# Grams made in turn for both heads, the state's steps put behind the inverse's products, and work placed anew between stages

## The reference

```python
def step(state, inp):                                  # 16 heads of 64, 512 tokens in order
    r_t, w_t, k_t, v_t, a_t, b_t = inp
    sa = jnp.einsum('bhvk,bhk->bhv', state, a_t)
    state = (state * w_t[:, :, None, :] + sa[..., None] * b_t[:, :, None, :]
             + v_t[..., None] * k_t[:, :, None, :])
    return state, jnp.einsum('bhvk,bhk->bhv', state, r_t)
# then, for each head and token:
y = (y - mean) * lax.rsqrt(var + GN_EPS) * ln_w + ln_b + bonus      # mean, var over the 64 of the head
out = y * g
```

## Time and profile before

| | |
|---|---|
| median of 3 runs | 3053.47 us (3048.03 to 3055.04) |
| the profiled execution | 3045.99 us, span 3044.2 us |
| TensorE busy | 2761.3 us (91%) |
| VectorE busy | 2143.8 us (70%) |
| ScalarE busy | 1238.6 us (41%) |
| GpSimd busy | 936.7 us (31%) |
| mean granted TensorE clock | 0.934 of full |

### The profile page before, as it was taken

One profiled execution on the slowest core, in us unless ns is written; L12 is line 12 of the kernel. 1 busy time (PEld: TensorE's weight loads), 2 busy tenths in 40 slices (PEclk: granted clock), 3 DMA queues, 4 the chain that ended last, 5 costly groups with the idle time before them and its releaser, 6 DMA issues. The chain is left out here.

```text
span 3044.2 us, 53724 instructions
## 1 busy us (share of the span) xinstructions
PE 2761.3 (91%) x20933; PEld 1742.6 (57%) x21115; DVE 2143.8 (70%) x3855; ACT 1238.6 (41%) x2050; POOL 936.7 (31%) x563
## 2 busy tenths in 40 slices
PE   8896998978999999999979999958888887889998
PEld 4443455655677777777745566636766664344444
DVE  6793469998788888888866367746667762577743
ACT  4333334478333333333340367634444432343321
POOL 0762344510555555555410222132333321000000
PEclk9657999999999999999989999978999988999999
DMA  4006434567999999999743322031111113623221
GB/s 143 28 1 220 151 118 149 178 243 276 385 374 365 365 359 358 367 364 363 260 152 95 96 74 60 16 137 35 57 34 34 35 55 125 240 83 111 84 104 49
DMA packets 277672, 513.25 MB, mean 169 GB/s; under 512 B 19376, under 2 KB 166448, under 8 KB 275312
## 3 DMA queue, kind: packets, MB, share of 16 engines
q1 hardware_dynamic: 240624, 376.48, 36.4%
q0 software_dynamic: 36864, 134.23, 11.3%
HBM read 445.05 MB, written 65.60 MB: 168 GB/s over the span
## 5 line engine op out<-in xcount | busy, mean ns | idle before, releaser
L1829 PE MATMUL banks<-gated_lo,v_hi 128*128 128x384 bf16 (+2 forms) x1536 | 335.0, 273 | 0.0
L1829 PE MATMUL banks<-gated_hi,v_lo 128*128 128x384 bf16 (+2 forms) x1536 | 335.0, 273 | 0.0
L1829 PE MATMUL banks<-gated_hi,v_hi 128*128 128x384 bf16 (+2 forms) x1536 | 335.0, 273 | 0.0
L1667 POOL DMA_INDIRECT gathered_u<-in_u_rows,first_tile_rows x128 | 212.3, 1659 | 299.2 <-DVE gathered_dots L1775 157.2
L1672 POOL DMA_INDIRECT gathered_v<-in_v,first_tile_rows x128 | 175.3, 1370 | 201.6 <-DVE x_tokens L1767 181.8
L2470 POOL MEMSET between<- 128x2048 bf16 x48 | 86.7, 1805 | 320.5 <-PE banks L3151 320.5
L1829 PEld LDWEIGHTS banks<-gated_hi,v_hi 128*128 128x128 bf16 x1536 | 150.2, 98 | 55.6
L1816 PE MATMUL banks<-act_hi,u_hi 128*128 128x384 bf16 x512 | 168.1, 328 | 12.0 <-DVE u_lo L1753 12.0
L1737 ACT CAST gated_hi<-gated 128x384 bf16<-128x384 f32 x128 | 65.5, 512 | 253.0 <-DVE gated L1789 242.0
L1767 DVE SCALAR_TENSOR_TENSOR x_tokens<-gathered_v,gathered_weights,x_tokens 128x1024 f32<-128x1024 f32 x128 | 164.1, 1282 | 6.1 <-issue 1.8
L1187 PE MATMUL banks<-act_hi,early_u_hi 128*128 128x384 bf16 x512 | 168.3, 329 | 0.0
(11 more groups left out here) (593 smaller groups left out, 7611.2 us busy)
## 6 DMA issues: line engine op xcount, KB each, us to landing
shared_room<-in_u SPq DMA_DIRECT2D x128, 512.0 KB, 3.9
shared_hi<-in_v SPq DMA_DIRECT2D x64, 512.0 KB
shared_lo<-in_v SPq DMA_DIRECT2D x64, 512.0 KB
gate_tables<-gate_piece SPq DMA_DIRECT2D x12, 2048.0 KB, 8.6
gate_group<-gate_tables SPq DMA_DIRECT2D x32, 768.0 KB
late_raw<-in_ffn_up SPq DMA_DIRECT2D x22, 1024.0 KB, 7.2
early_gelu<-early_gelu_columns SPq DMA_DIRECT2D x64, 192.0 KB, 1.9
gelu_early_rows<-early_gelu SPq DMA_DIRECT2D x32, 384.0 KB
```

The costliest lines, as they stand in the source:

```text
L1667: pool.indirect_dma_start(gu[:, n % GROUP, :], None, u_table, bass.IndirectOffsetOnAxis(ap=rows.index[:, 0, n:n + 1], axis=0)).then_inc(gu ...
L1829: m = pe.matmul(ps[:, bank, to:to + width], v[:, j, cols], w[:, j, tok:tok + width], start=start and n == 0 and to == 0, stop=stop and n = ...
```

## The change

1. **GateParts**: the 16 pieces are laid 2, 2, 3, 3, 6 beside chunks 1 to 5, where they were 6, 0, 2, 4, 4.
2. **NSA's output** is stored in eight pieces of two columns as they are made, not in two at the end.
3. **The squash block** is merged into `rwkv_heads`. SP issues the low-rank columns, then `load_pair(0)`, then the tables. TensorE waits for the squashed columns and for the tables only at `norm(0)`.
4. **Grams**: both heads of a gram in turn into two banks (head a SMALL, head b BETWEEN), behind `xlx` of level 2 (gram 1), 3 (gram 0) and 4 (gram 2). VectorE takes head b first. `lx` of levels 3, 4, 5 waits for that.
5. **State's steps**: part 2s-3 now stands behind `lx(s)` and part 2s-2 behind `xlx(s)`, on TensorE, and on ScalarE and VectorE behind the casts that belong to them. Part 11 stands at the end of the pass.
6. **The last pass's end** is done chunk by chunk between the state's steps (new part "last").

```diff
@@ GateParts
-        return {1: range(0, 6), 3: range(6, 8), 4: range(8, 12), 5: range(12, self.count)}.get(c, ())
+        return {1: range(0, 2), 2: range(2, 4), 3: range(4, 7), 4: range(7, 10), 5: range(10, self.count)}.get(c, ())
@@ rwkv_heads, sync
+                for n in range(RZ - 3 * KD):
+                    rows = min(P, RW_COLS - (3 * KD + n) * P)
+                    sp.dma_start(low_z[0:rows, n, :], k.dram["z"][3 * KD + n, 0:rows]).then_inc(low_landed, 16)
                 load_pair(0)
+                tables.load(k, sp)
@@ vector
-                def gram(j, g, h):
-                    steps.wait("rest", "tensor", j, f"gram{g}{'ab'[h]}")
+                def gram(j, g):
+                    steps.wait("rest", "tensor", j, f"gram{g}")
                     steps.wait("chain", "tensor", j - 2, f"y{NCH - 1}")
                     mark(1 + g)
                     mask = tri[:, min(g, 1), :].unsqueeze(1).to_broadcast([P, NCH, P])
+                    for h, bank in ((1, BETWEEN), (0, SMALL)):
+                        rest(dve.copy_predicated(G2[j % 2][:, g, h * NCH:(h + 1) * NCH], mask, by_chunk(ps[:, bank, :])),
+                             f"gram{g}{'ab'[h]}")
@@ vector, the passes
                         between_low(i, s)
+                        if chained and s > 1:
+                            chain(i - 1, 2 * s - 3)
...
-                            gram(i, 0, 1)
-                            gram(i, 2, 0)
...
+                        grown_low(i, s)
                         if chained:
                             chain(i - 1, 2 * s - 2)
-                        grown_low(i, s)
...
                         if s == 2:
+                            gram(i, 1)
                             if more:
                                 norms(i + 1)
-                            gram(i, 1, 1)
...
-                finish(KD - 1)
+                for c in CHUNKS:
+                    chain(KD - 1, 3 * c + 1)
+                    chain(KD - 1, 3 * c + 2)
+                    normed_chunk(c)
+                    if c + 1 < NCH:
+                        chain(KD - 1, 3 * c + 3)
+                    out_chunk(c)
@@ scalar, the passes
                         between_high(i, s)
+                        if chained and s > 1:
+                            chain(i - 1, 2 * s - 3)
...
+                        grown_high(i, s)
                         if chained:
                             chain(i - 1, 2 * s - 2)
-                        grown_high(i, s)
@@ tensor
-                def gram(j, g, h):
+                def gram(j, g):
                     left, right = ((kt, at2), (bt, rt2), (kt, rt2))[g]
                     for c in range(NCH):
                         cols = slice(c * P, (c + 1) * P)
+                        for h, bank in ((0, SMALL), (1, BETWEEN)):
+                            rows = slice(h * HD, (h + 1) * HD)
+                            ins = pe.matmul(ps[:, bank, cols], left[rows, cols], right[rows, j % 2, cols], start=True, stop=True)
@@ tensor, lx
+                    if s in (3, 4, 5):
+                        steps.wait("rest", "vector", i, f"gram{(1, 0, 2)[s - 3]}b")
@@ tensor, the passes
                         lx(i, s)
+                        if chained and s > 1:
+                            chain(i - 1, 2 * s - 3)
...
+                        xlx(i, s)
                         if chained:
                             chain(i - 1, 2 * s - 2)
-                        xlx(i, s)
...
                         dense(3)
-                        if chained:
-                            chain(i - 1, 2 * s - 1)
+                    if chained:
+                        chain(i - 1, 3 * NCH - 1)
@@ nsa_out_to_parts, sync
-            for n, part in enumerate((hi, lo)):
-                sp.wait_ge((high, low)[n], KD)
-                sp.dma_start(k.dram["nsa_parts"][:, n], part[:]).then_inc(stored, 16)
+            for d in range(0, KD, 2):
+                for n, part in enumerate((hi, lo)):
+                    sp.wait_ge((high, low)[n], d + 2)
+                    sp.dma_start(k.dram["nsa_parts"][:, n, d:d + 2], part[:, d:d + 2, :]).then_inc(stored, 16)
```

More of the change, by code:

```diff
@@ L2117 @@
 STAGES = 7
[L2120 to L2137, removed]
 LEVELS = range(1, STAGES)
@@ L2178, in rwkv_names @@
             "tensor": ["y_turned"],
+        },
+        "last": {
+            "scalar": [f"{n}{c}" for c in CHUNKS for n in ("squares", "gn_root", "out_hi")],
+            "vector": [n for c in CHUNKS for n in ("-", "-", f"centred{c}", "-", f"variance{c}", "-", f"normed{c}", "-", "-", f"out{c}", f"out_lo{c}")],
+            "tensor": [f"y_turned{c}" for c in CHUNKS],
         },
@@ L2966, in outs, with squares_and_root, high_chunk @@
                             branch_high(p + 2 - 2 * KD)
+                def squares_and_root(c):
+                    if c == 0:
+                        steps.begin("last", 0)
+                    two = slice(2 * c, 2 * c + 2)
+                    steps.wait("last", "vector", 0, f"centred{c}")
+                    steps.done("last", act.activation(ysq[:, c, :], yc[:, c, :], ACT.Square), f"squares{c}")
+                    steps.wait("last", "vector", 0, f"variance{c}")
+                    steps.done("last", act.activation(gn[:, 4, two], gn[:, 3, two], ACT.Sqrt), f"gn_root{c}")
+                def high_chunk(c):
+                    cols = slice(c * P, (c + 1) * P)
+                    steps.wait("last", "vector", 0, f"out{c}")
+                    steps.done("last", act.copy(oh[:, KD - 1, cols], o[:, cols]), f"out_hi{c}")
                 for part in range(3 * NCH):
@@ L2971, in _ @@
                     outs(part)
-                finish(KD - 1)
+                    c, what = divmod(part, 3)
+                    if what == 2:
+                        squares_and_root(c)
+                    if what == 1 and c >= 1:
+                        high_chunk(c - 1)
+                high_chunk(NCH - 1)
             @block.tensor
@@ L3060, in turn_k @@
                     steps.wait("first", "gpsimd", j, "kt")
-                    steps.wait("rest", "vector", j, "gram1b")
+                    steps.wait("rest", "vector", j, "gram1a")
                     if j + 1 < KD:
@@ L3263, in _, with turn_chunk @@
                         if s == 2:
-                            gram_1b(i)
+                            gram_1(i)
                         if s == 3:
-                            gram_0a(i)
+                            gram_0(i)
                         if s == 4:
-                            gram_2b(i)
+                            gram_2(i)
                         dense(3)
-                        if chained:
-                            chain(i - 1, 2 * s - 1)
+                    if chained:
+                        chain(i - 1, 3 * NCH - 1)
                     if more:
                         low_gram(i + 1)
+                def turn_chunk(c):
+                    if c == 0:
+                        steps.begin("last", 0)
+                        steps.wait("finish", "vector", KD - 2, "out")
+                    else:
+                        steps.wait("last", "vector", 0, f"out{c - 1}")
+                    steps.wait("last", "vector", 0, f"normed{c}")
+                    steps.done("last", pe.transpose(ps[:, SMALL, c * P:(c + 1) * P], yc[:, c, :], k.ident[:]), f"y_turned{c}")
                 for part in range(3 * NCH):
```

110 lines of the change are left out of this document (64 added, 46 removed).

## The result

The changed kernel takes 2971.1 us in the median (2969.3 to 2977.2), against 3053.1 for the kernel before on the same chip. The ratio is 0.9737, with a 95% interval of 0.9719 to 0.9756. It is faster, by 82 us in the medians. The two profiled executions stand 73.3 us apart (2972.6 and 3046.0), and this difference is what can be laid out by place.

A forecast was written before the change was run, and what follows sets the result against it. TensorE, busy 91%, was taken to lose time in idle stretches and at a lower clock. Gains 14 + 2.5 + 3.8 + 40 + 4 = 64.3 us took 3053.5 to 2989 us; own range 2977 to 3003, 8 in 10 2968 to 3015.

The forecast's parts named there:

- GateParts: TensorE's 16.41 us wait between `w_out` and `peer_wq`: `high(2)` and `low(2)` come sooner; gain 14 us, range 10 to 17.
- a gap that only moves: Rival at GateParts: `high(2)` stays held by its DMA or stores, so part 1 gives nothing; 3003 us, chance 0.06.
- NSA's stores: End of the NSA stage: storing in 256 KB pieces lets the next block's first DMA go sooner; gain 2.5 us (1 to 3).
- the squash block: First DMA to first RWKV matmul, 14.75 us: TensorE starts at 11 with the block merged; gain 3.8 us.
- The passes: Eight RWKV passes: paired Grams and moved state's steps take 54.1 us at full clock, 55.4 expected; gain 40 us, ends 15 and 52.
- half of the 2.5 us a pass: Middle passes: of 2.5 us a pass lost to TensorE's lower clock, half was kept as remaining, giving 55.4 us a pass.
- TensorE's new waits for VectorE's copies stay below 1 us: Sign in the passes: TensorE's wait moves from the gram to `lx` and is below 1 us each.
- The rival that ended slower: Passes: the twelve state's steps wait for their copies, 12 us more a pass; 3073 us, slower from 9.2 us a pass, chance 0.04.
- The last pass's end: After pass 7: chunked finish, inserted steps covered by 3.4 us of `dense` each; next block's DMA sooner, gain 4 us (2 to 5.5).
- emptying the banks may become the limit: Passes: if VectorE were the bound everywhere, they stay as they are; third rival, 3029 us, chance 0.07.

The follow-up runs named there:

- the last two kernels: Changed kernel with ScalarE's end order turned and VectorE's copies and unit keys earlier: 2958.8 us; then level 2's copies split around the state's step, GateParts piece later: 2952.7 us.

## Why the prediction was right, and where it was not

The forecast was 2989 us with its own range down to 2977. The result is below that, and inside the stated range. By its own steps:

- **GateParts (14; measured 15.2).** Each step of the working is found in the rows: `high(2)` at 275.15 for 274.0, the last piece cast by 283.75 for 282.7, the transposes at 287.90 for 286.9, and a clock that falls less (1.32 us for eight, not 1.97). So the start of the transposes gives 12.8 for 13.8, and the clock behind them brings the other 2.4, which the prediction had as a possibility only. In the trace `high(2)` is released by TensorE's product (L528), not by VectorE's taking of the bank. The rival of a gap that only moves is refuted by the kernel with this part alone.
- **NSA's stores (2.5; 3.2) and the squash block (3.8; 3.4).** The mechanism was right, and undoing both gave back about 6.5 us in their stretches, besides 2 us that belong to the clock and to a landing. The rule of the shared port pair (the Trainium skill, SBUF — State Buffer, Terms) agrees with three pairs of rows here: the cast of the masks takes 2.84 us beside a clear of GpSimd and 0.49 alone, the variance 1.66 us beside GpSimd's product, until that ends, and 0.17 alone, and the low part of a chunk 2.12 us and 0.29. The prediction used the rule for the first and did not ask where else the change would put the two engines side by side.
- **The passes (40; 53.4).** The mechanism and the lengths at full clock were right: 54.1 us was worked out for a pass, 53.75 measured. Levels 2, 3 and 4 were put at 8.3, 8.9 and 8.45 us, and take 8.54, 8.51 and 7.97. The mis-sized term is the clock. I kept half of the 2.5 us a pass, and a quarter of a microsecond is left. Without any of it my own sum gives 60.3 - 54.1 = 6.2 a pass, 37 for six, and 37.7 were measured. The reason I gave, the wait of 1.71 us going away, was too simple. The runs show that such a wait costs the clock among single Grams and mostly not among paired ones, and that either part of the change alone gives back most of it. For passes 0 and 7 (5 and 6; 7.5 and 8.3) the same term is likely, their clock having gone from 0.85 and 0.91 to 0.97 and 1.00; it was not taken apart there. The sign that TensorE's new waits for VectorE's copies stay below 1 us was missed: 1.30 us ahead of level 3, and 2.03 in pass 0.
- **What the state's steps bring.** The prediction costed Grams and steps together and did not say which gains. At full clock it is the Grams, 4.0 us a pass of 4.0. The steps' new place brings the clock if it stands alone, and 0.5 us a pass on top of the Grams. The rival that ended slower, from 9.2 us a pass, is far off: no wait of TensorE in passes 1 to 6 is longer than 1.7 us.
- **The last pass's end (4; -0.3).** This step failed: nothing was gained. It said that the inserted chunk steps are covered by 3.4 us of `dense` each, with up to 0.4 us lost once or twice, and that the last normalization is hidden by the last 16. The cover was cut by ScalarE's own order: it waits for those 16 products to evict them ahead of squaring, so the normalization begins when the cover ends, and three times falls beside GpSimd's work. The end did become 3.4 us shorter, and the stretch ahead of it 4.2 us longer, 0.9 of which it has with the old end too. Turning ScalarE's order round gives 4.6 us, and the end is then 3.9 us shorter than in the kernel before, which is what was forecast. That the kernel was faster than forecast all the same is owed to the passes, not to this step.
- **The rest.** 1.6 us more behind the stage were not forecast; they lie in a block that the change does not touch, and I did not find their cause. The medians differ by 82 us where the profiled executions differ by 73.3: the kernel before varied by 7 us from run to run in its group, and its passes alone can differ by 6 us through the clock, as the kernel with GateParts alone shows. So half of the 18 us between forecast and result lies in the places above and half in the executions compared.

The Trainium skill (TensorEngine Tiling (Array Packing), PSUM Bottleneck) warned that emptying the banks may become the limit. Each mask still takes 0.7 us for 1.16 us of both heads' products, but it was no bound: only the order in which VectorE took them was, 1.4 to 1.8 us a pass in the last two kernels.

## What to carry to other kernels

When two parts of a change remove the same idle time, cost each alone and both together; here 34 and 23 us alone made 38. Work laid under a cover is hidden only if every engine it passes through can start it while the cover lasts, so look at what stands ahead of it in that engine's order, the wait for the cover itself above all. Before a VectorE step is moved, look at what GpSimd does at the new time.

## What the runs showed of the hardware

- A granted clock that falls is not told by the length of one wait. A wait of 2.11 us among grams of both heads left it at 1.00 in four passes of six, and one of 2.03 us in pass 0 of the changed kernel at 1.00 from 2020 us on. One of 2.03 us among grams of one head brought a pass to 0.92 to 0.97 and the gram behind it from 1.16 to 2.07 us.
- Matmuls with 64 rows for the two halves of the array in turn: 16 take 1.16 us, as do 8 that all use one half.
- A VectorE operation on 128x2 numbers took 1.66 us beside a GpSimd product of 2.13 us, and a subtraction on 128x128 took 2.12 instead of 0.29. A sum over 128x128 right ahead of the first took its usual 0.29 beside the same GpSimd product; why it was not held is not shown.
